# Two-block transformer forward pass (attention, feed-forward, mLSTM mixer, band attention): turning 31 chunks with VectorE block transposes and DMA, retiming the mixer heads

## What is computed

```python
x = x + sliding_window_attention(rms_norm(x), ...)    # 32 query heads, 4 key/value heads
x = x + swiglu(rms_norm(x), w_gate, w_up, w_down)     # D_FF = 5632: 11 chunks of 512
# second block, layer 0: mLSTM mixer, 8 heads
h = modulate(rmsnorm(x, g_pre[0]), shift, scale)
proj = h @ w_in
qk = silu(causal_conv(proj[..., :A_V0], conv_w, conv_b))          # 4 taps along the rows
ht = rmsnorm(mlstm_chunkwise(q, k, v, li, lf))
y = (sigmoid(o) * ht * silu(z)) @ w_out
x = x + gate * rmsnorm(y, g_post[0])
# layer 1: keys and values from x, 16 heads of band attention, gate z, w_out
```

## Time and profile before

| what | value |
|---|---|
| median of 3 executions | 2404.92 us (2404.87 to 2405.07) |
| profiled execution, its own time | 2404.78 us |
| its span in the profile | 2403.0 us |
| mean granted TensorE clock | 0.999 |
| PE busy | 2384.5 us (99%) |
| VectorE busy | 1747.5 us (73%) |
| ScalarE busy | 1312.8 us (55%) |
| DMA moved | 578.14 MB, 241 GB/s |

### The profile page before, as it was taken

The page is one execution under the profiler, slowest core; times in us unless marked ns, Lnnn a source line. Parts: engine busy times, 40 slices in busy tenths (PEclk is TensorE's granted clock), DMA queues, the critical chain, the costliest instruction groups (busy, mean ns, idle before and its releaser), DMA issues.

```text
span 2403.0 us, 30577 instructions
## 1 busy us (share of the span) xinstructions
PE 2384.5 (99%) x11017; PEld 1944.2 (81%) x11017; DVE 1747.5 (73%) x2438; ACT 1312.8 (55%) x1913; POOL 44.3 (2%) x67
## 2 busy tenths in 40 slices
PE   9999999999999999999999999999999999999998
PEld 7777888888888888778888888888888778888887
DVE  8885778677787776668778677677776676666665
ACT  6665465545563555545545544555455576655553
POOL 1100000000000000000000000000000000000000
PEclk9999999999999999999999999999999999999999
DMA  8445888788889896567777787777777557776654
GB/s 298 146 132 172 269 294 308 256 305 301 286 313 311 286 316 229 163 222 242 240 238 232 244 273 241 239 239 236 243 245 239 155 186 264 251 240 215 227 194 136
DMA packets 161830, 578.14 MB, mean 241 GB/s; under 512 B 18288, under 2 KB 20592, under 8 KB 161680
## 3 DMA queue, kind: packets, MB, share of 16 engines
q1 hardware_dynamic: 160432, 572.64, 71.5%
q0 software_dynamic: 1104, 3.28, 0.5%
q10 hardware_dynamic: 144, 0.26, 0.0%
HBM read 574.01 MB, written 2.10 MB: 240 GB/s over the span
## 4 chain that ended last, share of the span: by engine, by line
PE 94%; DVE 2%; ACT 2%; issue 1%; DMA 1%; POOL 0%; SPq 0%; DVEq 0%; ACTq 0%
PE PS L1173 30%; PE PS L1175 30%; PE PS L1174 30%; DVE WL L2219 1%; ACT WH L1570 1%; PE PS L916 1%; DMA X<-in_x 0%; PE PS L811 0%; PE PS L884 0%; DVE X L2186 0%; PE PS L1006 0%; PE PS L1074 0%; PE PS L1026 0%; PE PS L1027 0%; PE PS L1023 0%
## 5 line engine op out<-in xcount | busy, mean ns | idle before, releaser
L2219 DVE TENSOR_TENSOR WL<-W,WH 128x1024 fp32r<-128x1024 f32 x814 | 988.9, 1222 | 506.4 <-ACT WH L1570 500.1
L1570 ACT ACTIVATE WH<-W 128x1024 fp32r<-128x1024 f32 x814 | 854.9, 1058 | 720.4 <-PE PS L1175 682.5
L1173 PE MATMUL PS<-WH,XTH 128*128 128x512 f32 x2144 | 853.5, 398 | 3.2 <-DVE XTL L1725 1.2
L1175 PE MATMUL PS<-WH,XTL 128*128 128x512 f32 x2144 | 835.7, 390 | 0.0
L1174 PE MATMUL PS<-WL,XTH 128*128 128x512 f32 x2144 | 835.2, 390 | 0.0
L1173 PEld LDWEIGHTS PS<-WH,XTH 128*128 128x128 f32 x2144 | 402.8, 188 | 93.8 <-issue 10.4
L1175 PEld LDWEIGHTS PS<-WH,XTL 128*128 128x128 f32 x2144 | 402.4, 188 | 85.4
L1174 PEld LDWEIGHTS PS<-WL,XTH 128*128 128x128 f32 x2144 | 402.9, 188 | 83.7 <-issue 3.8
L1173 PE MATMUL PS<-WH,YTH 128*128 128x512 f32 x1120 | 440.2, 393 | 3.5 <-DVE WL L2219 2.4
L1175 PE MATMUL PS<-WH,YTL 128*128 128x512 f32 x1120 | 436.1, 389 | 0.0
L1174 PE MATMUL PS<-WL,YTH 128*128 128x512 f32 x1120 | 436.0, 389 | 0.0
(11 more groups left out here) (287 smaller groups left out, 1182.2 us busy)
## 6 DMA issues: line engine op xcount, KB each, us to landing
W<-in_vec SPq DMA_DIRECT2D x192, 512.0 KB, 4.4
W<-in_avoz SPq DMA_DIRECT2D x192, 512.0 KB, 4.5
W<-in_wg SPq DMA_DIRECT2D x88, 512.0 KB, 5.1
W<-in_wu SPq DMA_DIRECT2D x88, 512.0 KB, 4.8
W<-in_wd SPq DMA_DIRECT2D x88, 512.0 KB, 4.9
W<-in_gate SPq DMA_DIRECT2D x64, 512.0 KB, 4.4
W<-in_aqk SPq DMA_DIRECT2D x64, 512.0 KB, 4.4
W<-in_aout SPq DMA_DIRECT2D x64, 512.0 KB, 4.4
```

The source lines that it names most:

```text
L1173: e.matmul(p, x, WH[:, g % NH, j], start=first, stop=False)
L1175: i = e.matmul(p, y, WH[:, g % NH, j], start=False, stop=last)
L1570: e.activation(WH[:, n % NH], W[:, i % NW], ACT.Copy).then_inc(s_hi, 1)
L2219: e.tensor_tensor(l, src, h.bitcast(F32), ALU.subtract).then_inc(s_lo, 1)
```

## The change

- `blocks_T` lays the transposed blocks out so that, for each pair of a source and a target quadrant, they form 32 partitions of 1 KB. SP's program then copies TQ to MT by 16 DMAs of 32 KB per chunk (`carry`), in two parts of eight with one weight load between; `carry_points` places them in the sequence of loads. `quadrants` is gone.
- The query/key chunk of each mixer head is turned the same way: 11 + 16 + 4 = 31 chunks, 496 DMAs. ScalarE copies the turned chunk from MT to QK4, and the convolution reads it from there. PE's turns (`four_turns` on QK) are gone.
- `M2` and `nsel` have 128 rows instead of 64; M2's rows are filled by VectorE instead of ScalarE.
- In the mixer head the steps move: convolution parts at ticks 11, 13, 15, 17 (before 6, 7, 9, 10), decay at 14 (before 11, in head 0 14), query-key product at 26 (before 17), denominators at 32 (before 23). In `gates` three ticks stand before "gate_c".
- Scaled low parts (mixer outputs) are made in eight pieces of 128 x 128 instead of four of 128 x 256.

```diff
-MT_FFN, MT_MIX = 0, 11
-TQ_FFN, TQ_MIX, TQ_KEYS = 0, 11, 19
-
-MV = {k: i + 1 for i, k in enumerate("qk cva cvb qm pm vv den q2 nv0 nv1 z0 y0 z1 y1".split())}
-MA = {k: i + 1 for i, k in enumerate("qk sg ee vv sn0 sn1 o0 o1 z".split())}
+TQ_FFN, TQ_MIX, TQ_KEYS = 0, 11, 27
+TURNED = {"ffn": (19,), "mix": (3, 52), "keys": (3,)}
+
+MV = {k: i + 1 for i, k in enumerate("qk cva cvb vv qm pm den q2 nv0 nv1 z0 y0 z1 y1".split())}
...
+def carry_points(plan):
+
+
+    points, due = {}, []
+    tick = low = number = 0
+    for what, *a in score(plan):
+        if what in ("slot", "lower", "fold"):
+            low = max([low] + list(plan.lower[a[0]]))
+        elif what == "start" and a[0] in TURNED:
+            due += [tick + n for n in TURNED[a[0]]]
+        elif what == "tick":
+            tick += 1
+            while tick in due:
+                due.remove(tick)
+                number += 1
+                for part in range(2):
+                    points.setdefault(low + NW + 1 + part, []).append((number, part))
+    return points
+
...
-        M2 = sb("M2", [64, 384], F32R)
-        nsel = sb("nsel", [64, 8], F32R)
-        MT = sb("MT", [128, 4, 256])
-        TQ = sb("TQ", [128, 2, 512])
+        M2 = sb("M2", [128, 384], F32R)
+        nsel = sb("nsel", [128, 8], F32R)
+        MT = sb("MT", [128, 4, 4, 2, 32])
...
+        def feature_blocks(j, n):
+
+            return MT[:, :, j:j + n].rearrange("p a j t r -> p (j t) a r")
+
+        def by_quadrant(T, k0, n):
+
+            return T[:, k0:k0 + n].rearrange("p k (t a r) -> p (k t) a r", t=2, a=4)
...
-                yield
+                yield from ticks(3)
                 b, full = take("gate_c")
...
-                yield from ticks(4)
-                for half in range(2):
-                    b, full = take(("qkT", h, half))
-                    w.wait_ge(s_mixa, ata("qk"))
-                    w.wait_ge(s_mix, at("qk"))
-                    four_turns(b, lambda j, t: QK[:, t, 128 * (2 * half + j):128 * (2 * half + j) + 128], full)
-                    yield from ticks(2)
-                    give(("qkT", h, half), s_mix, at("cva" if half == 0 else "cvb"))
-                    yield
+                yield from ticks(13)
                 b, full = take(("decay", h))
-                yield from ticks(0 if h else 3)
                 w.wait_ge(s_mm, 2)
                 w.wait_ge(s_nsel, 4)
-                e.matmul(b[:, 0:384], nsel[:, h:h + 1].to_broadcast([64, 128]), M2[:], start=True, stop=False)
+                e.matmul(b[:, 0:384], nsel[:, h:h + 1].to_broadcast([128, 128]), M2[:], start=True, stop=False)
                 e.matmul(b[:, 0:512].rearrange("p (a c k) -> p a c k", a=2, c=2)[:, :, 0], idb[:],
                          mcT[:].unsqueeze(1).to_broadcast([128, 2, 128]), start=False, stop=True).then_inc(full, 1)
                 give(("decay", h), s_mixa, ata("ee"))
-                yield from ticks(6 if h else 3)
+                yield from ticks(6)
+                gfree[ends[1][0]] = [(s_mixa, ata("vv")), (s_mix, at("vv"))]
+                yield from ticks(6)
                 b, full = take(("qk", h))
                 w.wait_ge(s_mix, at("qm"))
                 for f in range(2):
@@ -1007,11 +1029,9 @@
                     i = e.matmul(b[:, 256:384], QM[:, 2 + f, 128:256], QM[:, f, 128:256], start=False, stop=(f == 1))
                 i.then_inc(full, 1)
...
-                w.wait_ge(s_mix, at("vv"))
+                w.wait_ge(s_mix, at("pm"))
...
-            def quadrants(number, dst, n, sem):
-
-                w.wait_ge(s_tq, number)
-                for x in range(16):
-                    a, b = slice(32 * (x // 4), 32 * (x // 4) + 32), x % 4
-                    o = dst[32 * b:32 * b + 32].rearrange("p j (t r) -> p t j r", t=2)[:, :, :, a]
-                    i = e.activation(o, TQ[a].rearrange("p t (j b r) -> p t j b r", j=4, b=4)[:, :, :, b], ACT.Copy)
-                    if x == 15:
-                        i.then_inc(sem, 1)
-                    if x % n == n - 1:
-                        yield
-
             def pairs_T(number, k0, scale):
 
-                w.wait_ge(s_mt, number)
+                w.wait_ge(s_mt, 256 * number)
                 for x in (0, 2):
                     if scale is None:
-                        i = e.activation(YTH[:, k0 + x:k0 + x + 2], MT[:, x:x + 2], ACT.Copy)
+                        i = e.activation(by_quadrant(YTH, k0 + x, 2), feature_blocks(x, 2), ACT.Copy)
                     else:
                         for j in (x, x + 1):
-                            i = e.activation(YTH[:, k0 + j], MT[:, j], ACT.Copy, scale=scale(k0 + j))
+                            i = e.activation(by_quadrant(YTH, k0 + j, 1), feature_blocks(j, 1), ACT.Copy,
+                                             scale=scale(k0 + j))
                     i.then_inc(s_yh, 1)
                     yield
...
-                yield from ticks(19)
-                yield from quadrants(TQ_FFN + f + 1, MT, 4 if f == 10 else 2, s_mt)
+                yield from ticks(25)
                 w.wait_ge(s_unit, free)
-                yield from pairs_T(MT_FFN + f + 1, 4 * slot, None)
+                yield from pairs_T(TQ_FFN + f + 1, 4 * slot, None)
...
-                yield from ticks(10)
-                w.wait_ge(s_mix, at("cvb"))
+                yield from ticks(9)
+                w.wait_ge(s_mt, 256 * (TQ_MIX + 2 * h + 1))
+                e.activation(by_quadrant(QK4, 0, 4), feature_blocks(0, 4), ACT.Copy).then_inc(s_qkl, 1)
+                yield from ticks(8)
+                w.wait_ge(s_unit, ends[1][1])
                 if h:
                     w.wait_ge(s_mix, at("y1", h - 1))
...
-                yield from quadrants(TQ_KEYS + j + 1, KT[:, 4 * j:4 * j + 4], 2, s_kq)
+                w.wait_ge(s_mt, 256 * (TQ_KEYS + j + 1))
+                e.activation(by_quadrant(KT, 4 * j, 4), feature_blocks(0, 4), ACT.Copy).then_inc(s_kq, 1)
+                yield
...
-            def blocks_T(src):
-
-                for t in range(2):
-                    i = e.transpose(TQ[:, t], src[:, t])
+            def blocks_T(number, src):
+
+                if number > 1:
+                    w.wait_ge(s_mt, 256 * (number - 1))
+                for t in range(2):
+                    i = e.transpose(TQ[:, :, :, t].rearrange("p b j r -> p j b r"),
+                                    src[:, t].rearrange("p (j b r) -> p j b r", j=4, b=4))
                     if t:
                         i.then_inc(s_tq, 1)
...
+                            for t in range(2):
+                                h, l = (Y[:, k0 + j, 128 * t:128 * t + 128].rearrange("p (a r) -> p a r", a=4)
+                                        for Y in (YTH, YTL))
+                                i = e.scalar_tensor_tensor(out=l, in0=MT[:, :, j, t], scalar=scale(k0 + j),
+                                                           in1=h.bitcast(F32), op0=ALU.mult, op1=ALU.subtract)
...
+                e.tensor_copy(M2[0:8, 0:256], MM)
+                e.tensor_copy(M2[0:8, 256:384], MM[:, 128:256]).then_inc(s_mm, 1)
...
-                    b = full(("qkT", h, half))
+                    w.wait_ge(s_qkl, h + 1)
                     wcol = 2 * h + j + 16 * half
-                    u, o = b[:, 256 * j:256 * j + 256], CV[:, 2 * half + j]
+                    u, o = QK4[:, 2 * half + j], CV[:, 2 * half + j]
                     wt = [cols[:, CCW + 32 * q + wcol:CCW + 32 * q + wcol + 1] for q in range(4)]
...
-                yield from ticks(5)
+                yield
+                w.wait_ge(s_mixa, ata("qk"))
+                w.wait_ge(s_mix, at("qk"))
+                yield from blocks_T(TQ_MIX + 2 * h + 1, QK)
+                yield from ticks(7)
                 conv(0, 0)
-                yield
+                yield from ticks(2)
                 conv(0, 1)
                 yield from ticks(2)
                 conv(1, 0)
-                yield
+                yield from ticks(2)
                 conv(1, 1)
                 yield
+                par, g = ends[1]
+                w.wait_ge(s_unit, g)
+                e.tensor_copy(VV[:, 1], Gb[par][1][:, :]).then_inc(s_mix, 1)
...
+            points = carry_points(plan)
+
+            def carry(number, part):
+
+                w.wait_ge(s_tq, number)
+                if number > TQ_KEYS + 1:
+                    w.wait_ge(s_kq, number - TQ_KEYS - 1)
+                for a in (2 * part, 2 * part + 1):
+                    for b in range(4):
+                        e.dma_start(MT[32 * b:32 * b + 32, a].rearrange("p j t r -> p (j t r)"),
+                                    TQ[32 * a:32 * a + 32, b].rearrange("p j t r -> p (j t r)")).then_inc(s_mt, 16)
+
             for i, (kind, what, src) in enumerate(stream):
+                for number, part in points.get(i, ()):
+                    carry(number, part)
                 if i == 0:
                     e.dma_start(cols[:, 0:32], A["cols"][:, 0:32]).then_inc(s_gain, 16)
```

(11 more changed lines are left out.)

71 lines of the change are left out of this document (29 added, 42 removed).

## The result

The changed kernel took a median of 2486.21 us (2484.91 to 2487.68, 4 runs) against 2404.89 of the kernel before: a ratio of 1.0337, 95% interval 1.0324 to 1.035, 81 us slower. The forecast was 2395.0, the range ended at 2416.

The account below looks back on a forecast made before the run. The prediction took PE's own stream and its rare waits as the bound: 2404.78 us less gains of 11.4 (7.0, 1.7, 1.6, 0.3, 0.8) gives 2393.4, plus 1.6 for the carry's stalls makes 2395.0 us; range 2391.5 to 2416.

Parts of the forecast that it names:

- the turns: PE's identity matmuls on the mixer's query/key chunks: 16 groups at 0.435 us each removed, -7.0 us.
- the decay rows: Decay group in each of eight mixer heads: padding to 128 rows saves 0.215 us each, -1.7 us (0 to -2.8).
- The waits of L1006 and L969: PE's waits at head 0's query-key product and at the gate: later ticks remove them, -1.6 and -0.3 us.
- The 0.8 us after the last feed-forward chunk: PE's stall before the last chunk's down projection goes with ScalarE's quadrant copies: -0.8 us (0 to -1.3).
- The pace of the carry: SP's queue: 0.40 us per issue (0.37 to 0.475), 17 issues taking 6.8 us per chunk.
- L: Time a mixer head's query/key carry has landed: T + 7.0 + 6.8 + 2.2 = T+16.0.
- T: Time at which a mixer head's query/key chunk ends and its head's program starts; 1102.81 us in head 1 before.
- T+7.0: When TQ is ready in a mixer head; put at T+7.0 to T+8.8, the early end taken.
- Rival 1: The carry decides, at ScalarE's QK4 copy and VectorE's queue behind it: slower, 2414.4 us (2410 to 2420); chance 0.28.
- the stall at WL of unit 12: PE in each mixer head stalls by what L exceeds T+15.8: 0.2 us a head, +1.6 us (none to +26).
- Hidden: Feed-forward and key chunks: blocks land by 310.4 to 312.2, before first YTH at 313.12; +1 us at most.
- just covered: Weight loads late by up to 4 us between the carry's parts, 8 behind it; slots leave 7.8 us of room.

Follow-up runs that it names:

- f1: The changed kernel with 8 instead of 16 transfers per chunk, the same 32 KB each, chunk 0 whole, half the data left out: 2398.5 us.
- e1: The kernel before with only the decay operands M2 and nsel padded from 64 to 128 rows: 2402.95 us, ratio 0.9992.
- f3: The changed kernel, all work done, with GpSimd issuing the second eight transfers of each chunk beside SP's first eight: 2408.78 us, ratio 1.0017.
- g2: The changed kernel with the 32-partition transfers to MT reading x in DRAM instead of TQ (wrong data): 2425.32 us.
- f2: The changed kernel with 16 transfers per chunk of 16 KB instead of 32 KB, chunk 0 whole, half the data left out: 2483.68 us.
- e3: The changed kernel without the transfers of the eight mixer outputs, their data left out, the wait for TQ kept: 2448.45 us.
- f4: The changed kernel with ScalarE's and VectorE's pairs of feed-forward chunks 8 ticks later, except the last chunk of each of three groups: 2471.73 us.
- g1: The changed kernel with the same number of 32 KB transfers, each between 128 partitions of TQ and MT (blocks misplaced): 2485.94 us.
- g4: f3 with nine transfers per chunk on SP and seven on GpSimd, descriptor memory as before: 2402.50 us, ratio 0.999.
- i1: f3 with GpSimd issuing 11 of 16 transfers per feed-forward chunk, 7 per query/key chunk, 5 per mixer output, 8 per key chunk: 2424.09 us, ratio 1.008.
- h1: f3 with nine transfers on SP, seven on GpSimd, and GpSimd's descriptor memory enlarged to 7168 bytes: 2404.71 us, ratio 0.9999.
- g3: f3 with GpSimd's descriptor memory enlarged from 4096 to 7168 bytes: 2404.02 us, ratio 0.9996.

## Why the prediction was wrong

**What bounds it, and the gains: right.** -7.0 for the turns and -2.3 for the decay rows are what f1's 9.0 us of PE's busy time bear out. The decay group gave -2.3 where the sum had -1.7: what was mis-sized is the 0.08 us that I added for the step after it: the group costs what its 640 columns cost (0.75 less 0.455 is 0.30, I had 0.37). The rule that a load goes by its columns, which the Trainium skill gives (TensorE: Matmul & The Clock Gate, LDWEIGHTS (loading the stationary operand)), agrees with the load's length of 182 against 187 ns, and yet padding the rows paid, as e1's rows show: the length of a load is not all it costs. The waits of L1006 and L969 went. The 0.8 us after the last feed-forward chunk did not go in the changed kernel, whose carry stalls there; in f3, where it does not, that stage is 1.6 us shorter.

**The pace of the carry: the step that failed first.** "What one issue costs the queue is between two rows", 0.37 and 0.475, and I took 0.40. It is 0.63, outside both bounds. The bounds came from rows whose source is in DRAM, and g2 shows that for such a source they were right (0.42 and 0.04 between). No row showed a transfer with both ends in SBUF, and the bound should have been left open upward for that. The carry took 10.7 us instead of 6.8 (f1, f2). The rule of the Trainium skill that starting a transfer is usually small beside the transfer (DMA: Bandwidth & Descriptors, Issuing engines are not separate DMA queues) holds here for one transfer, 0.59 against a landing of 2.4 us, but not for sixteen in a row, whose starts take 9.5 us.

**The mixer output's carry: not priced.** I worked out L from the query/key chunk alone and took TQ at T+7.0 "as those copies are gone". ScalarE's copies before had at least let a WH pass between every few of them; the wait that replaces them lets none pass. TQ came at T+10.2, beyond the upper bound of T+8.8, and e3 puts 37.8 us on it. Rival 1 named the right place, ScalarE's QK4 copy and what stands behind it, and had 20 us for it.

**Where PE stands first: wrong unit.** I had the stall at WL of unit 12 and a threshold of T+15.8. In head 2 PE stood at unit 8, for WH and its WL, where the threshold is T+18.5 (T+21.8 less the copy and one WH, 2.1 us, and one WL, 1.2). The copy started 4.6 us behind it, and PE waited 4.45. In f1 that copy starts at about T+15, and PE does not wait in that head. The threshold of unit 12 was not tested by itself.

**The price of a stall: too low.** I charged the idle time alone. Each wait also cost 0.3 us of run-out, and eight of them were followed by the lower clock, some 13 us in all. The 92 us of stalls are 62 of idle time and 30 of these two, on which the sum had nothing.

**"Hidden" in the feed-forward stage: wrong, 26.9 us.** I compared the landing with the time at which YTH was made before. But a wait at the head of an engine's queue costs what stands behind it. Before, ScalarE spent the time ahead of YTH on short copies with WH between them; now it stood for 8.0 us with WH behind it. And of the weight loads behind the carry I wrote "just covered", 7.8 us of room against 7.6 of delay at the pace of 0.475; at 0.63 they are not, but f4 shows that this is the smaller part, 5.0 of 22.1 us in the chunks that it moves.

## What to carry to other kernels

A wait put in place of work on an in-order engine costs what is queued behind it, even if the result comes no later than before: ask what could pass earlier and can't now. Price a transfer by its issues on the queue, from a row with the same source and target; when the trace has none, leave that bound open, and ask what the queue's other loads lose meanwhile. Price a stall of TensorE above its idle time: here a third of the loss was run-out and lower clock. Two queues side by side took nearly all of the cost away, and that was the experiment worth making before the change.

## What was not expected of the hardware

- Issuing a 32 KB transfer to SBUF on SP, right behind another, takes 0.59 us when its source is in SBUF too and 0.42 when it is in DRAM; into an idle queue 0.51 and 0.33, and a store from SBUF to DRAM 0.33. The number of partitions (32 or 128) and the bytes (16 or 32 KB) don't matter (g1, g2, f2). On GpSimd it takes 0.50 (f3).
- GpSimd stood 3.4 to 6.0 us after 106 to 118 transfers and again 85 transfers later (f3, g4, i1), and with more descriptor memory first after 149 and 152 (h1, g3). That the descriptor memory was full is what fits; the profile shows only "issue".
- After some waits of TensorE of 1.8 us or more the granted clock stood at 1.2 GHz for 3.4 us, once 6.8, and matmuls of 512 columns started 0.427 us apart instead of 0.227 (changed kernel, eight times).
- A load of 64 rows among loads of 128 made its group of matmuls 0.29 us longer, though by itself it took 182 ns against 187 (e1).
